# Weight tiles split into high and low parts two at a time, one more weighted one-hot per eight on ScalarE, eight expert rows moved ahead

## What is computed

```python
s1 = jnp.einsum('thd,hnd->thn', q[..., :half], sub_keys[:, 0])
s2 = jnp.einsum('thd,hnd->thn', q[..., half:], sub_keys[:, 1])
v1, i1 = lax.top_k(s1, P_TOPK)
v2, i2 = lax.top_k(s2, P_TOPK)
...
vals, ci = lax.top_k(cand, P_TOPK)
e = i1[...] * N_KEYS + i2[...]          # the experts of a token
g = jax.nn.softmax(vals, axis=-1)       # their gates
...
a = jnp.einsum('cd,ckd->ck', xc, expert_u[ec])
w = gc * jax.nn.gelu(a)
y = jnp.einsum('ck,ckd->cd', w, expert_v[ec])
```

## Time and profile before

| | us |
|---|---|
| median of 3 runs | 2191.14 (2191.01 to 2192.11) |
| the profiled execution | 2191.93 |
| its span in the profile | 2190.2 |
| PE busy | 2123.4 (97%) |
| DVE busy | 1650.5 (75%) |
| ACT busy | 1044.8 (48%) |
| DMA engines, mean | 221 GB/s |

### The profile page before, as it was taken

One profiled execution on the slowest core, in us unless ns is written; L12 is line 12 of the kernel. 1 busy time (PEld: TensorE's weight loads), 2 busy tenths in 40 slices (PEclk: granted clock), 3 DMA queues, 4 the chain that ended last, 5 costly groups with the idle time before them and its releaser, 6 DMA issues.

```text
span 2190.2 us, 33425 instructions
## 1 busy us (share of the span) xinstructions
PE 2123.4 (97%) x11713; PEld 1787.9 (82%) x11713; DVE 1650.5 (75%) x3228; ACT 1044.8 (48%) x1940; POOL 635.8 (29%) x425
## 2 busy tenths in 40 slices
PE   7999999999999988899999989999998999999999
PEld 6888888888888545687899988999997888888887
DVE  6555555534367687554399999999988999999998
ACT  5333333322243477744455535999844433333332
POOL 0000000000040000020100223777626767767773
PEclk9999999999999999999999999999999999999999
DMA  5322222222325200022355888999989999999996
GB/s 195 97 86 86 86 86 92 82 97 98 98 97 182 78 1 1 1 68 87 125 170 178 281 259 291 377 410 400 395 304 417 419 418 418 418 419 418 419 418 278
DMA packets 137228, 484.57 MB, mean 221 GB/s; under 512 B 15056, under 2 KB 30416, under 8 KB 135184
## 3 DMA queue, kind: packets, MB, share of 16 engines
q1 hardware_dynamic: 75456, 229.93, 29.8%
q0 software_dynamic: 59056, 225.14, 26.0%
q10 hardware_dynamic: 2592, 27.85, 3.1%
HBM read 435.42 MB, written 46.92 MB: 220 GB/s over the span
## 4 chain that ended last, share of the span: by engine, by line
PE 79%; DVE 17%; ACT 2%; issue 1%; DMA 0%; ACTq 0%; DVEq 0%
PE bank L1257 24%; PE bank L495 15%; PE bank L496 15%; PE bank L497 15%; DVE rows L2327 5%; DVE wlo L482 3%; DVE hot L2485 2%; PE bank L510 2%; DVE hot L2483 2%; PE bank L610 1%; PE bank L570 1%; PE bank L813 1%; PE bank L831 1%; ACT pair_prob L1479 1%; PE bank L1211 1%
## 5 line engine op out<-in xcount | busy, mean ns | idle before, releaser
L495 PE MATMUL bank<-act_hi,whi 128*128 128x320 f32 (+1 forms) x1840 | 646.6, 351 | 23.2 <-DVE wlo L482 19.8
L496 PE MATMUL bank<-act_lo,whi 128*128 128x320 f32 (+1 forms) x1840 | 635.3, 345 | 0.0
L497 PE MATMUL bank<-act_hi,wlo 128*128 128x320 f32 (+1 forms) x1840 | 635.0, 345 | 0.0
L482 DVE TENSOR_TENSOR wlo<-raw,whi 128x1024 fp32r<-128x1024 f32 x398 | 486.0, 1222 | 140.4 <-ACT whi L478 138.2
L478 ACT ACTIVATE whi<-raw 128x1024 fp32r<-128x1024 f32 x398 | 417.9, 1056 | 341.4 <-PE bank L1257 203.9
L495 PEld LDWEIGHTS bank<-act_hi,whi 128*128 128x128 f32 x1840 | 346.2, 188 | 65.6 <-DVE wlo L482 23.4
L497 PEld LDWEIGHTS bank<-act_hi,wlo 128*128 128x128 f32 x1840 | 346.0, 188 | 32.8
L496 PEld LDWEIGHTS bank<-act_lo,whi 128*128 128x128 f32 x1840 | 346.4, 188 | 31.6 <-issue 0.7
L762 POOL DMA_INDIRECT rows<-peer_u,idxU x128 | 194.4, 1519 | 330.7 <-DVE udot L2327 158.8
L1257 PE MATMUL bank<-whi,h_hi 128*128 128x512 f32 x768 | 237.9, 390 | 7.2 <-issue 7.2
L1257 PE MATMUL bank<-wlo,h_hi 128*128 128x512 f32 x768 | 237.8, 390 | 0.0
(11 more groups left out here) (403 smaller groups left out, 2929.2 us busy)
## 6 DMA issues: line engine op xcount, KB each, us to landing
raw<-tiles SPq DMA_DIRECT2D x398, 512.0 KB, 4.9
gates_dram<-stage ACTq DMA_DIRECT2D x12, 2048.0 KB, 11.3
wg<-gates_dram POOLq DMA_DIRECT2D x16, 1536.0 KB, 17.1
acts_dram<-gelu SPq DMA_DIRECT2D x120, 160.0 KB, 5.0
hf<-acts_dram POOLq DMA_DIRECT2D x30, 640.0 KB, 13.5
bias<-alibi POOLq DMA_DIRECT2D x16, 256.0 KB, 3.0
w1s<-cmp_w POOLq DMA_DIRECT2D x1, 4096.0 KB, 12.9
res<-x_t ACTq DMA_DIRECT2D x4, 512.0 KB, 6.7
```

The lines of the kernel that those rows point to most:

```text
L482: dve.tensor_tensor(wlo[:, j.slot, :], raw[:, j.slot, :], whi[:, j.slot, :].bitcast(F32), ALU.subtract).then_inc(lo_made, 1)
L495: pe.matmul(to, wh, x, start=(kc == 0), stop=False)
L496: pe.matmul(to, wh, xl, start=False, stop=False)
L497: last = pe.matmul(to, wl, x, start=False, stop=(kc == KC - 1))
```

## The change

Three things. High and low parts are made for two neighbouring tiles by one instruction of 128 x 2048 in all expert jobs but U2 and U3, whose high parts stay single (their low parts are a pair). In the first 40 pieces of the gates ACT makes five of eight weighted one-hots (tokens 1, 2, 3, 6, 7 of a piece) and DVE three. And `DOTS_GATES` is 84, not 76, so eight more rows are used beside the gates and eight fewer beside the V jobs.

```diff
-DOTS_GATES = 76
+DOTS_GATES = 84
...
+        def make_two_hi(act, j):
+            two = slice(j.slot, j.slot + 2)
+            for slot in (j.slot, j.slot + 1):
+                act.wait_ge(raw_landed[slot], (j.turn + 1) * 16)
+            act.wait_ge(job_done, j.n + 2)
+            act.activation(whi[:, two, :], raw[:, two, :], ACT.Copy).then_inc(hi_made, 2)
+
+        def make_two_lo(dve, j):
+            two = slice(j.slot, j.slot + 2)
+            dve.wait_ge(hi_made, j.n + 2)
+            dve.tensor_tensor(wlo[:, two, :], raw[:, two, :], whi[:, two, :].bitcast(F32),
+                              ALU.subtract).then_inc(lo_made, 2)
...
-                    pe.wait_ge(S("hot2_made"), min(2 * gi + 2, 4 * EXTRA_Q))
+                    pe.wait_ge(S("hot2_made"), min(5 * q + 3 + gi % 2 * 2, 5 * EXTRA_Q))
...
             def u_job(n, ahead=AHEAD):
                 j = Job(J_U + n)
-                make_hi(act, j.ahead(ahead))
+                if n == 0:
+                    make_hi(act, j.ahead(ahead))
+                elif n % 2:
+                    make_two_hi(act, j.ahead(ahead))
                 activation_of(j, n // RING)
...
-                spots = [(gi, x) for gi in (2 * q, 2 * q + 1) for x in (2, 3)]
+                spots = [(2 * q, x) for x in (1, 2, 3)] + [(2 * q + 1, x) for x in (2, 3)]
...
-                if jj + HI_AHEAD < P:
-                    make_hi(act, Job(J_V + jj).ahead(HI_AHEAD))
+                if jj % 2 and jj + HI_AHEAD < P:
+                    make_two_hi(act, Job(J_V + jj).ahead(HI_AHEAD))
...
             def u_job(n):
-                make_lo(dve, Job(J_U + n).ahead())
+                if n % 2 == 0:
+                    make_two_lo(dve, Job(J_U + n).ahead())
...
-                for x in (0, 1, 4, 5) if q < EXTRA_Q else range(8):
+                for x in (0, 4, 5) if q < EXTRA_Q else range(8):
...
-                make_lo(dve, Job(J_U + U_GATES + q).ahead())
+                if q % 2 == 0:
+                    make_two_lo(dve, Job(J_U + U_GATES + q).ahead())
...
-                if jj + AHEAD < P:
-                    make_lo(dve, Job(J_V + jj).ahead())
+                if jj % 2 == 0 and jj + AHEAD < P:
+                    make_two_lo(dve, Job(J_V + jj).ahead())
```

More of the change, by code:

```diff
@@ L1640, in weighted_hot @@
                     t = gate_tokens(gi) + x
-                    act.wait_ge(S("hot_apart"), 4 * q + at_ + 1)
+                    act.wait_ge(S("hot_apart"), 5 * q + at_ + 1)
                     act.activation(hot[:, gi % 4 * 4 + x, 1, :], hot[:, gi % 4 * 4 + x, 1, :], ACT.Relu,
@@ L2492, in _ @@
             for n in range(KEPT):
-                make_lo(dve, Job(J_U + U_REST + n).ahead())
+                if n % 2 == 0:
+                    make_two_lo(dve, Job(J_U + U_REST + n).ahead())
                 for _ in range(DOTS_REST * n // KEPT, DOTS_REST * (n + 1) // KEPT):
```

## The result

The changed kernel takes 2215.01 us (median of 5 runs, 2212.7 to 2218.94), the kernel before 2191.14; the ratio is 1.0109, 95% interval 1.0095 to 1.0123. That is slower, as forecast, but by 23.9 us and not by 9.4, and outside the range of 2194 to 2212. The profiled execution is the slowest of the five, 2218.94 us with a span of 2217.2, so its stages add up to 27.0 us more than those of the earlier trace rows, not to 24.

What follows compares the result with a forecast made beforehand. PE was taken to bound the kernel, with DVE second beside selection and gates. U2 1.1, selection 2.5, gates 6.8 and -1.0 behind them sum to +9.4 us on the median 2191.14, giving 2200.5; range 2194 to 2212.

Steps and rivals of the forecast that it cites:

- Gates, +6.8 at U112, -1.0 behind: 40 gate pieces: ACT's piece 5.73 us against PE's 5.32, U112 6.8 us later; 1.0 less PE waiting for DVE behind them.
- rival 5: Selection and gates: selection loses 5 us and semaphores cost ACT 2 more; 2205 to 2209, chance 0.08.
- Rival 3: Gates: ACT takes the fifth one-hot in idle time and DVE's relief counts, -2.4 to -8 us; 2185, chance 0.07.
- The double instructions and U2: Pairs take 2.30 us on DVE and 1.90 on ACT; in the selection U2 starts 1.1 us late on PE.
- 0.16 on both engines: Upper bound on a double instruction's saving on DVE and ACT: all that a single row takes beyond its slope.
- Selection, +2.5: Selection after U2: lost DVE lead costs 2.0 us, pairs give 0.8 back, earlier blocks lose 1.3; between 0 and 5.
- The blocks before end with PE and DVE nearly even: Selection, token blocks before the last: a loss of 1.3 us for both together.
- the lead of U44: Selection: DVE's low-part lead at U44 falls from 5.8 us to at most 2.7, with 2.0 lost.
- each block loses 2: Selection: upper bound of 5 us on the stage's loss, if every token block loses 2.
- V jobs and the rest: 0: V jobs and remaining stages: no loss; lead capped at 3.8 us, V116's low part as a pair still 0.4 early.
- Rival 2: V jobs: double buffering by pairs too short, each second pair 1 us late, 32 us in all; 2215, chance 0.12.
- rivals 1: Whole kernel: the terms as summed hold, own range 2196 to 2206 us; chance 0.68.

Runs made afterwards that it cites:

- rest_single: The changed kernel with single high and low parts for U112 to U127; +13.6 us over the kernel before.
- five_84: The changed kernel without any pair: ACT makes five of eight one-hots, 84 rows; +7.2 us against the kernel before.
- third: The kernel before with ACT making the fifth one-hot in every third piece of the gates, no pairs, 76 rows; -4.3 us.
- half_inner: The kernel before with ACT's fifth one-hot in every second piece of the gates and pairs for U76 to U111, 76 rows; -6.4 us.
- v_early: The kernel before with pairs for V0 to V31 only; +1.6 us.
- v_late: The kernel before with pairs for V48 to V127 only; +1.0 us, no difference within its interval.
- after: The changed kernel itself, against the kernel before; 2215.01 us, ratio 1.0109.
- pairs_76: The changed kernel's pairs everywhere, but four of eight one-hots on ACT and 76 rows as in the kernel before; +22.0 us against the latter.
- pairs_sel: The kernel before with pairs only for U2 to U71 (U4 to U71 on ACT), four one-hots and 76 rows; +6.5 us.
- pairs_v: The kernel before with pairs only for V0 to V127, four one-hots and 76 rows; +3.8 us.
- third_v0: The kernel before with ACT's fifth one-hot in every third piece of the gates and the single pair V0, V1, 76 rows; -4.5 us.
- third_both: The kernel before with ACT's fifth one-hot in every third piece, pairs for U76 to U111 and the pair V0, V1, 76 rows; -5.4 us.

## Why the prediction was wrong

**Gates, +6.8 at U112, -1.0 behind: right.** Measured +8.1 and -0.7. Four pieces take 22.9 us, as summed, so the 0.05 a piece for semaphores that rival 5 adds isn't there. The 1.3 more lie at the entry, where U73 starts 1.5 us later than before relative to U72. That is the clock: U72 ran 6.8 us at a mean of 0.75, and in rest_single, with the same wait ahead of it but the clock at 1.00, the gates cost +6.0. ACT's debt is shown by five_84 (+7.2 without any pair) and by its other side, third and half_inner: with the fifth one-hot in every third or every second piece (there with pairs) it is a gain. Rival 3's mechanism was real at a third of the dose. The advice of the Trainium skill, Perfetto Trace Analysis, "Optimizing Scalar/DVE Operations", that handing work of a saturated DVE to Scalar may make sense, is borne out here at a smaller dose only. With a mean ACT piece of 5.33 us (third, by the sum) or 5.39 (half_inner) the kernel gained, with 5.78 (five_84) it lost. Between them no run tells where the gain ends; a piece took 5.52 us before.

**The double instructions and U2: right.** 2286 and 1916 ns; U2 1.2 us late against 1.1. (The bound "0.16 on both engines" holds for DVE; for ACT the same rows give 0.21.)

**Selection, +2.5: mis-sized; measured +10.9 (9.1 to 13.6 in the three kernels with this code).** The step that failed is "The blocks before end with PE and DVE nearly even, and I take 1.3 for both together". I worked out what I took for the last block, from rows of two: the lead of U44 belongs to the third block (U34 to U52), PE's 8.3 us of waits to the fourth. In the fourth, between U56 and U68, nothing was lost at all. The blocks before lost 9.6 from U4 to U52: 2.4 us at U22 and U23, 1.4 at U32, 4.3 between U48 and U52, the rest in small steps. DVE has time there in the first half of a block and none in the second, and lives on its lead; I looked only at the lead of U44, and the cap of 2.4 us there (2.7 summed) was right. (That all even U jobs would have 2.7 at most, as the prediction's signs say, was not: U4 has 7.2, and in the gates they have 7.7.) Two more things were missing from the sum. PE's waits in the stage grew by 7.1 us (from 12.1 to 19.1), but the stage by 10.9: behind three of the waits (2.7 us at U22, 3.8 at U50, 2.9 at U58) the job ran at a mean clock of 0.82, 0.67 and 0.67 and took about 1.5 us longer each, which more than makes up the other 3.8. And at U46 ACT waited 2.7 us for a load. A pair frees two buffers late and at once; the load of U47 was issued at 1243.95 and landed 11 us later:

```profile
1255.36 1.91 ACT L490 ACTIVATE whi<-raw 128x2048 fp32r<-128x2048 f32 x1 [2.69 <-DMA raw<-tiles]
```

My bound of 5 ("each block loses 2") had the same fault: it took the 2 of my mixed block for the measure of all, while the third alone lost 4.3 at its end.

**"V jobs and the rest: 0": wrong twice.** *The start of V, +3.9:* I costed U112 to U127 at nothing without naming what stands behind the first pair on DVE: the rows, on which V0 waits. rest_single shows the price of the pairs U112 to U127, 6.0 us; the pair V0, V1 gives 2 back. *The V jobs, +4.5:* the cap was right (3.8 summed, 3.6 measured), and with it I asked whether V116's pair would still be in time with DVE standing where it stood, 1.5 us ahead of PE. But DVE stood there only because it had been 9.7 us ahead up to V42 and had spent 8 since, waiting for rows among other things. With the cap it has 3.6 to spend. The waits of DVE and the one it led to in the changed kernel, V100 on PE:

```profile
DVE own L2349 <- DMA rows<-peer_v,idxU: 20.4, 12, 3.6
```

```profile
2093.95 1.28 DVE L2349 SCALAR_TENSOR_TENSOR own<-rows,udot,own 128x1024 f32<-128x1024 f32 x1 [3.63 <-DMA rows<-peer_v,idxU]
2095.98 1.28 DVE L2349 SCALAR_TENSOR_TENSOR own<-rows,udot,own 128x1024 f32<-128x1024 f32 x1 [0.74 <-DMA rows<-peer_v,idxU]
2097.18 2.28 DVE L495 TENSOR_TENSOR wlo<-raw,whi 128x2048 fp32r<-128x2048 f32 x1
```

```profile
2099.52 0.73 PE L1270 MATMUL bank<-whi,h_hi 128*128 128x512 f32 x2 [2.81 <-DVE wlo L495]
```

Before, DVE waited for late rows as well (10.9 us for those of `peer_v`), and no such wait reached PE. Now two of them, 4.4 us, go through a lead of some 2 to PE. The changed kernel's runs lie 6 us apart and those before 2; late rows and the clock behind waits both differ between executions, and how much each has of the 6 isn't shown. Rival 2 named double buffering as too short, but by late loads of `raw`; here ACT waited 6.9 us for those in all, and it was the rows. Its number, 2215, is the measured median by luck: its mechanism isn't what happened, and its own "32 us in all" doesn't lead to it. (The chances have a slip too: rivals 1, 2 and 5 alone are 0.88, above the 0.87 for slower.)

v_early shows that the lead isn't won back once it is cut, and v_late's trace that it costs nothing until it is used up. How much of a V loss is DVE's own work and how much late rows isn't settled; it changes from run to run.

## What to carry to other kernels

Before you make two steps' worth of an operand at once, read the lead (end of the operand to start of its user) over the whole stage, not where it is smallest: a lead of 9 us that shrinks to 1.5 at the end is spent time, and capping it early takes it away at the end. Look at what is queued behind the wider instruction on its engine and who waits for that; inside a steady stage with lead to spare the same pair gained what it saved. And when an engine has 0.2 us to give in each piece and a unit of work costs 0.7, hand over a unit in every third piece rather than in each: the edit went from +7.2 (with eight rows moved as well) to -4.3 us.

## What was unexpected of the hardware

A long wait of PE costs more than its length, but not each time. After a wait of 3.8 us U50 took 5.15 us instead of 3.52, at a mean granted clock of 0.67. After 2.7 us U22 took 8.5 us at 0.82 (after), 9.8 at 0.69 (pairs_76) and 7.1 at 1.00 (pairs_sel, rest_single); after 3.0 us U72 took 6.8 at 0.75 (after) and 5.3 at 1.00 (rest_single, pairs_76). One and the same wait in the same code was followed by the lower clock in one execution and not in another. From U0 on, in the traces of all the kernels, this is so for waits of 1.9 to 3.0 us; the job behind each longer one, up to 12.7, ran in part at the lower clock. In the kernel before, the longest wait between U0 and U127 was 2.2 us, and the clock stayed at 1.00 in the selection and the gates.

A row used later can let the stage end earlier: with DVE using the rows ahead of it later, V0 started 2.0 to 2.3 us earlier after U116, in five kernels out of five that have the pair V0, V1 and single parts ahead of it (pairs_v, v_early, third_v0, third_both, rest_single: 58.0 to 58.3 us, against 60.3 before). That it is so because fewer gathers then share the queue with the last one is likely by the traces, not shown.
